# The banded-attention section issued two steps at a time, with its value and score matmuls next to each other

## The chip, the cores and the metric

The kernel runs on one core of a Trainium2 chip. The metric is device time in microseconds (us), from one execution; lower is better. TensorE does the matmuls, VectorE, ScalarE and GpSimd work beside it, and SyncE issues the loads of the weights. Each engine takes its instructions in the order in which they are written, and waits for the others by semaphores.

## The reference

The program is a whole model: two layers of one kind of block, then two layers of another. The change touches one part, the attention of the last layer, which looks 128 tokens to either side (512 tokens, 16 query heads, 4 key heads, head width 64, float32):

```python
def window_gqa_mixer(h, wqkv, wo, sink, cos, sin):
    qkv = h @ wqkv
    ...
    o, _ = band_attention(q, k, v, B_RADIUS, B_BLOCK, sink.reshape(B_KV_HEADS, grp))
    return o.reshape(b, s, B_HEADS * D_HEAD) @ wo

# band_attention, for one query block of 128 and its neighbours
s = jnp.einsum('nbqhgd,nbkhd->nbhgqk', qb, kb) * (dh ** -0.5)
s = jnp.where(valid, s, NEG_INF)
m = jnp.maximum(jnp.max(s, axis=-1), sk)
pr = jnp.exp(s - m[..., None])
den = jnp.sum(pr, axis=-1) + jnp.exp(sk - m)
o = jnp.einsum('nbhgqk,nbkhd->nbqhgd', pr, vb) / den
```

## The kernel before

The section (`mixer_b`) has two kinds of work for TensorE. The *dense* work multiplies the 512 tokens by weights: a tile of 128 outputs takes 8 pieces (4 in the last phase), a piece is three matmuls of 512 columns (L913 to L915), and the weights of each 8 pieces are a *unit*. The first 96 pieces make the tiles k0, v0, q0, q1, k1, q2, q3, v1, q4 to q7; the next 32 are the first half of the output projection. When a tile is done, VectorE takes it out of its bank: a rope tile by a shuffle and a product (L2704, L2705), after which GpSimd does two more operations on it (L842, L843). At the end of each unit ScalarE makes the high part of a later unit's weights (L1645) and VectorE the low part (L2146).

The *banded* work is 32 steps `s` of two heads (`g` = 0, 1) and one query tile `t = s % 4`. `b_blocks(s)` gives its key blocks: two at t = 0 and 3, three at t = 1 and 2. A step has these stages:

- `scores`: TensorE, one float32 matmul for each head, 256 or 384 columns, on 64 rows of the array each, into banks 2 and 3 (even s) or 4 and 5 (odd s); then VectorE adds the mask, takes the row maximum (L2746) and makes the bias of the exponential (L2827).
- `exps`: ScalarE, one exponential for each head, in place in `scb` (L2033).
- `norm`: VectorE, a reciprocal (L2770) and two scalings (L2772).
- `blocks`: TensorE transposes (L1537) into the one bank 6, four of them in one group at two key blocks, two groups of three at three; ScalarE copies each group to `ptb` (L2059), and the next group waits for that copy.
- `values`: TensorE, 8 or 12 instructions (L1551), 64 columns of the array for each head, into bank 7. After every fourth step ScalarE and VectorE take bank 7 out in two parts (`out`, `out_lo`).

The order is written out by hand in the generator `plan_b` (L304), which every engine walks for itself, taking the stages that are its own. `dense.send(n)` issues n pieces, with the events "unit" and "part" where a unit or a half tile ends. Before step 0, 46 pieces are out; the 32 steps issue the other 82. In front of the loop VectorE still takes out tile k1 behind `scores` 1. `rest` (the second half of the output projection) follows.

`ptb` is one buffer, so that a copy waits for the values of the step before; `scb` and the small statistics have three.

Of the kernel before, what the change touches and what calls it, by code (L numbers as in the profile page):

```python
# [21 lines left out]
ALU = mybir.AluOpType  # L22
# [281 lines left out]
def plan_b():  # L304


    dense = woven(len(B_TILES), B_PART, lambda d: B_TILES[d][0] == "v", BY_THREE)
    next(dense)
    yield from dense.send(40)
    yield "scores", 0  # L310
    yield "exps", 0
    yield from dense.send(3)
    yield "norm", 0
    yield "scores", 1
    yield from dense.send(3)
    for s in range(32):
        if s % 4 == 0 and s:
            yield "out_lo", s // 4 - 1
        if s == 0:
            yield "blocks", (0, 0)  # L320
            yield "exps", 1
        if s < 30:
            yield "scores", s + 2
        if s:
            yield "blocks", (s, 0)
        if s < 31:
            yield "norm", s + 1
        n = 3 if s % 3 and s not in (25, 28, 31) else 2
        if len(b_blocks(s)) == 3:
            yield from dense.send(1)  # L330
            yield "blocks", (s, 1)
            yield from dense.send(n - 1)
        else:
            yield from dense.send(n)
        if s < 30:
            yield "exps", s + 2
        yield "values", s
        if s % 4 == 3:
            yield "out", s // 4
# [70 lines left out]
def build(nc, stream, x_t, p_t, small, vecs, tab1, tab_a, tab_b, consts, out):  # L410
    n_units = stream.shape[0]
    with ExitStack() as ctx:
# [81 lines left out]
        scb = [at(f"scb{i}", [P, 2, 3 * P + 8], offset=o + i * (6 * P + 16) * 4) for i in range(3)]; o += 3 * (6 * P + 16) * 4  # L494
        ptb = at("ptb", [P, 6 * P], offset=o); o += 6 * P * 4
# [16 lines left out]
        mxs = at("mxs", [P, 3, 2, 2])  # L512
        nms = at("nms", [P, 3, 2])
        dns = at("dns", [P, 3, 2])
        rdn = at("rdn", [P, 3, 2])
        nsink = at("nsink", [P, 16])
        sink8 = at("sink8", [P, 16])
        eps = at("eps", [P, 2])
# [132 lines left out]

        def b_scores(s, g):

            return scb[s % 3][:, g, (3 - len(b_blocks(s))) * P:3 * P]

        block = ctx.enter_context(nc.Block())

# [249 lines left out]
        def _(pe):  # L907
# [621 lines left out]
            def blocks_b(s, i):  # L1529

                nb = len(b_blocks(s))
                if i == 0:
                    c.wait(p_scaled)
                dst = group_bank()
                for j in range(4 if nb == 2 else 3):
                    g, k = divmod(j, 2) if nb == 2 else (i, j)
                    mm = pe.transpose(dst[:, chunk(j)], b_scores(s, g)[:, chunk(k)], ident[:, :])  # L1537
                mm.then_inc(grp_done, 1)

            def values_b(s):  # L1540

                qc, t = divmod(s, QT)
                nb = len(b_blocks(s))
                pe.wait_ge(grp_read, c.n["group"])
                if t == 0:
                    pe.wait_ge(o_lo, 4 + qc)
                if s == 0:
                    evicted(4)
                for k, kt in enumerate(b_blocks(s)):
                    for g in range(2):  # L1550
                        mm = pe.matmul(bank[7][rows(g), chunk(t)], bv[qc // 4][:, kt, rows(g)], ptb[:, chunk(nb * g + k)],  # L1551
                                       start=k == 0, stop=k == nb - 1, skip_group_check=True)
                mm.then_inc(v_done, 1)

# [77 lines left out]
        def _(act):  # L1632
# [358 lines left out]
            def exps_a(s):  # L1991

                act.wait_ge(m_ready, s + 1)
                for g in range(2):
                    sc = sca[s % 2][:, g, :]
                    act.activation(sc, sc, ACT.Exp, bias=nms[:, s % 3, g:g + 1], scale=0.125,
                                   accum_out=dns[:, s % 3, g:g + 1]).then_inc(e_done, 1)

            def mixer_a():
                c.start(banks_mixer)  # L2000
# [27 lines left out]
            def exps_b(s):  # L2028

                act.wait_ge(m_ready, 16 + s + 1)  # L2030
                for g in range(2):
                    sc = scb[s % 3][:, g, (3 - len(b_blocks(s))) * P:3 * P + 1]
                    act.activation(sc, sc, ACT.Exp, bias=nms[:, s % 3, g:g + 1], scale=0.125,  # L2033
                                   accum_out=dns[:, s % 3, g:g + 1]).then_inc(e_done, 1)

            def mixer_b():
                c.start(banks_mixer)
                for stage, k in plan_b():
                    if stage == "unit":
                        unit_over()  # L2040
                        if k < len(B_TILES):
                            c.next_tile()
                        split_after(k, AFTER_NORM)
                    elif stage == "part":
                        c.next_tile()
                    elif stage == "turn":
                        c.tick("group")
                        act.wait_ge(grp_done, c.n["group"])
                        act.activation(bv[int(B_TILES[k][1])][:, :, :], bank[6][:, :].rearrange("p (t d) -> p t d", t=QT),
                                       ACT.Copy).then_inc(grp_read, 1)  # L2050
                    elif stage == "exps":
                        exps_b(k)
                    elif stage == "blocks":
                        s, i = k
                        w = (4 if len(b_blocks(s)) == 2 else 3) * P
                        c.tick("group")
                        act.wait_ge(grp_done, c.n["group"])
                        act.wait_ge(v_done, 16 + s)
# [78 lines left out]
        def _(dve):  # L2137
# [612 lines left out]
            def scores_a(s):  # L2750

                if s == 0:
                    c.wait(mask_in, 16)
                dve.wait_ge(s_done, s + 1)
                if s >= 2:
                    dve.wait_ge(grp_done, c.n[f"step{s - 2}"])
                for g in range(2):
                    masked(sca[s % 2][:, g, 0:S], bank[2 + g][:, :], tba[:, A_M0 + s % QT * S:A_M0 + s % QT * S + S],
                           mxs[:, s % 3, g, 0:1])
                    masked(sca[s % 2][:, g, S:S + 2 * P], bank[4 + g][:, 0:2 * P], tba[:, A_M1:A_M1 + 2 * P],  # L2760
                           mxs[:, s % 3, g, 1:2])
                for g in range(2):
                    ins = dve.tensor_scalar(nms[:, s % 3, g:g + 1], mxs[:, s % 3, g, 0:1], mxs[:, s % 3, g, 1:2], -0.125,
                                            ALU.max, ALU.mult)
                ins.then_inc(m_ready, 1)

            def norm(s, n, sc):

                dve.wait_ge(e_done, 2 * (n + s + 1))
                link(dve.reciprocal(rdn[:, s % 3, :], dns[:, s % 3, :]))  # L2770
                for g in range(2):
                    ins = dve.tensor_scalar(sc(g), sc(g), rdn[:, s % 3, g:g + 1], None, ALU.mult)  # L2772
                ins.then_inc(p_scaled, 1)

            def mixer_a():
# [36 lines left out]
            def scores_b(s):  # L2812

                qc, t = divmod(s, QT)
                nb = len(b_blocks(s))
                h0 = qc // 4 * 8 + qc % 4
                if s == 0:
                    c.wait(mask_in, 16)
                dve.wait_ge(s_done, 16 + s + 1)
                if s >= 3:  # L2820
                    dve.wait_ge(grp_done, c.n[f"step{s - 3}"])
                dve.tensor_reduce(scb[s % 3][:, :, 3 * P], sink8[:, h0:h0 + 5:4].unsqueeze(2), AX.X, ALU.max)
                for g in range(2):
                    masked(b_scores(s, g), bank[2 + 2 * (s % 2) + g][:, 0:nb * P],
                           tbb[:, B_M + (b_blocks(s)[0] - t + 1) * P:B_M + (b_blocks(s)[0] - t + 1 + nb) * P],
                           mxs[:, s % 3, g, 0:1])
                dve.scalar_tensor_tensor(nms[:, s % 3, :], mxs[:, s % 3, :, 0], -0.125, nsink[:, h0:h0 + 5:4],  # L2827
                                         ALU.mult, ALU.min).then_inc(m_ready, 1)

            def mixer_b():  # L2830
# [281 lines left out]
```

## Time and profile before

| | us |
|---|---|
| median of 3 runs | 3358.89 (3358.5 to 3358.99) |
| the profiled execution | 3358.6 |
| its span in the profile | 3356.6 |

| engine | busy, us of the span |
|---|---|
| TensorE (PE) | 3310.1 |
| VectorE (DVE) | 1818.7 |
| ScalarE (ACT) | 1244.5 |
| GpSimd (POOL) | 332.5 |

Times in the profile are microseconds from the first instruction. The length of a matmul in it includes a tail that overlaps the next one, so what a matmul costs is read from one start to the next start. The 32 banded steps run from 2765.09 us (transposes of step 0) to 2895.29 us (first piece of `rest`), 130.20 us.

### The profile page before, as it was taken

The numbers are of one execution on the slowest core, as the hardware profiler recorded it, in microseconds if no ns is written. First come the engines' busy times: TensorE is split into PE (matmuls) and PEld (weight loads), VectorE is DVE, ScalarE is ACT, GpSimd is POOL, SyncE is SP. The second block draws the span as 40 slices with busy tenths as digits, with TensorE's granted clock in tenths as the row PEclk, the third lists the DMA queues.
The fourth block names the chain that finished last, engine by engine and source line by source line (L and its number), as shares of the span: only waits on it lengthen the run. The fifth ranks groups of instructions, "written<-read, shape, count | busy, mean of one in ns | idle before, by whom it ended". The sixth has DMA issues, their size and how long they took to land.

```text
span 3356.6 us, 43153 instructions
## 1 busy us (share of the span) xinstructions
PE 3310.1 (99%) x16870; PEld 2645.2 (79%) x16870; DVE 1818.7 (54%) x2946; ACT 1244.5 (37%) x1882; POOL 332.5 (10%) x242
## 2 busy tenths in 40 slices
PE   9999999999999999999999999999999999999999
PEld 7767888776788878888777778888888876788887
DVE  6776333677743446443666664436644367654436
ACT  3355232425532324232333343224433235532325
POOL 0300000231100020000223100001000012000001
PEclk9999999999999999999999999999999999999999
DMA  4112222321122222223322122233222321132332
GB/s 166 63 45 80 96 95 99 126 69 45 62 96 95 100 94 84 98 94 107 109 70 70 64 88 94 100 102 106 82 94 100 102 96 45 57 107 94 100 107 82
DMA packets 81433, 300.39 MB, mean 89 GB/s; under 512 B 9040, under 2 KB 9040, under 8 KB 80640
## 3 DMA queue, kind: packets, MB, share of 16 engines
q1 hardware_dynamic: 78624, 284.20, 25.2%
q0 software_dynamic: 1568, 11.98, 0.9%
q8 instruction: 105, 1.72, 0.2%
q10 hardware_dynamic: 1088, 2.10, 0.2%
q14 instruction: 48, 0.39, 0.0%
HBM read 296.14 MB, written 2.10 MB: 89 GB/s over the span
## 4 chain that ended last, share of the span: by engine, by line
PE 90%; DVE 4%; ACT 3%; issue 1%; POOL 1%; DMA 0%; POOLq 0%; ACTq 0%; DVEq 0%
PE bank L913 26%; PE bank L915 25%; PE bank L914 25%; PE bank L957 2%; PE bank L964 2%; PE bank L958 2%; PE bank L1241 1%; PE bank L1222 1%; PE bank L1482 1%; PE bank L1494 1%; DVE wl L2146 1%; ACT wh L1645 1%; PE bank L1537 1%; ACT sc L1817 1%; PE bank L1256 1%
## 5 line engine op out<-in xcount | busy, mean ns | idle before, releaser
L913 PE MATMUL bank<-x,wh 128*128 128x512 f32 x2616 | 1043.9, 399 | 3.1 <-DVE wl L2146 1.8
L915 PE MATMUL bank<-x,wl 128*128 128x512 f32 x2616 | 1020.0, 390 | 0.0
L914 PE MATMUL bank<-x,wh 128*128 128x512 f32 x2616 | 1018.8, 389 | 0.0
L1645 ACT ACTIVATE wh<-raw 128x1024 fp32r<-128x1024 f32 x526 | 556.8, 1059 | 1114.5 <-PE bank L915 1062.5
L2146 DVE TENSOR_TENSOR wl<-raw,wh 128x1024 fp32r<-128x1024 f32 x526 | 669.9, 1274 | 534.0 <-ACT wh L1645 533.1
L913 PEld LDWEIGHTS bank<-x,wh 128*128 128x128 f32 x2616 | 491.3, 188 | 122.5 <-issue 22.6
L915 PEld LDWEIGHTS bank<-x,wl 128*128 128x128 f32 x2616 | 491.0, 188 | 104.2
L914 PEld LDWEIGHTS bank<-x,wh 128*128 128x128 f32 x2616 | 491.8, 188 | 99.3 <-issue 3.8
L913 PE MATMUL bank<-mid,wh 128*128 128x512 f32 x1216 | 474.9, 391 | 0.5 <-DVE wl L2146 0.5
L914 PE MATMUL bank<-mid,wh 128*128 128x512 f32 x1216 | 473.1, 389 | 0.0
L915 PE MATMUL bank<-mid,wl 128*128 128x512 f32 x1216 | 473.1, 389 | 0.0
L913 PEld LDWEIGHTS bank<-mid,wh 128*128 128x128 f32 x1216 | 228.3, 188 | 49.7 <-DVE wl L2146 1.3
L914 PEld LDWEIGHTS bank<-mid,wh 128*128 128x128 f32 x1216 | 228.3, 188 | 48.4 <-issue 1.0
L915 PEld LDWEIGHTS bank<-mid,wl 128*128 128x128 f32 x1216 | 228.3, 188 | 47.1
L2290 DVE TENSOR_TENSOR prod<-bank,rs_in 128x512 f32<-128x512 f32 x88 | 60.8, 691 | 233.2 <-PE bank L915 233.2
L2162 DVE TENSOR_TENSOR mid<-prod,mid 128x512 f32 (+1 forms) x152 | 104.8, 689 | 89.7 <-ACT mid L1958 86.9
L710 POOL TENSOR_TENSOR acc<-sq,sq 128x512 f32<-128x512 f32 x8 | 11.2, 1396 | 1283.9 <-ACT sq L1762 1283.9
L2628 DVE TENSOR_TENSOR prod<-tmp,bank 128x512 f32<-128x512 f32 x64 | 44.0, 687 | 142.7 <-ACT tmp L1908 142.7
L1958 ACT ACTIVATE mid<-prod 128x512 f32 (+1 forms) x88 | 55.8, 634 | 174.7 <-DVE prod L2676 174.7
L1908 ACT ACTIVATE tmp<-bank 128x512 f32<-128x512 f32 x64 | 38.3, 598 | 177.9 <-PE bank L915 177.9
L957 PE MATMUL bank<-x,wh 128*128 128x512 f32 x200 | 80.3, 401 | 13.5 <-DVE wl L2146 7.0
L2290 DVE TENSOR_TENSOR tmp<-bank,rs_in 128x512 f32<-128x512 f32 x88 | 60.8, 691 | 56.9 <-PE bank L915 55.8
(377 smaller groups left out, 3323.3 us busy)
## 6 DMA issues: line engine op xcount, KB each, us to landing
raw<-stream SPq DMA_DIRECT2D x526, 512.0 KB, 3.2
raw_apart<-stream SPq DMA_DIRECT2D x12, 512.0 KB, 3.6
sm<-small POOLq DMA_DIRECT2D x2, 2144.0 KB, 9.7
tb<-tab POOLq DMA_DIRECT2D x2, 1728.0 KB, 13.9
h<-x_t ACTq DMA_DIRECT2D x4, 512.0 KB, 6.8
out_t<-h SPq DMA_DIRECT2D x8, 256.0 KB, 2.7
tba<-tab_a POOLq DMA_DIRECT2D x1, 1152.0 KB, 8.1
pf<-p_t POOLq DMA_DIRECT2D x2, 512.0 KB, 5.4
```

Source lines behind the costliest of these rows:

```text
L913: pe.matmul(dst, hi, src[:, kc, 0, :], start=start, stop=False)
L914: pe.matmul(dst, hi, src[:, kc, 1, :], start=False, stop=False)
L915: return pe.matmul(dst, lo, src[:, kc, 0, :], start=False, stop=stop)
L957: pe.matmul(dst, hi, x[:, kc, 0, :], start=kc == 0, stop=False)
L958: pe.matmul(dst, lo, x[:, kc, 0, :], start=False, stop=False)
L964: mm = pe.matmul(dst, hi, x[:, kc, 1, :], start=False, stop=kc == 7)
L1645: act.activation(high_of(n)[:, :], raw_of(n)[:, :], ACT.Copy).then_inc(hi_done, 1)
L1958: act.activation(mid[:, i * 2 + k, 0, :], prod[k][:, :], ACT.Copy).then_inc(mid_hi, 1)
L2146: dve.tensor_tensor(low_of(n)[:, :], raw_of(n)[:, :], high_of(n)[:, :].bitcast(F32), ALU.subtract).then_inc(split_done, 1)
L2162: dve.tensor_tensor(dst, src, hi.bitcast(F32), ALU.subtract).then_inc(done, 1)
L2290: free(dve.tensor_tensor(dst, bank[c.peek()][:, :], rs_in[:, :], ALU.mult))
L2628: free(dve.tensor_tensor(prod[k % 2][:, :], tmp[k % 2][:, :], b[:, :], ALU.mult))
```

## The change

The loop of `plan_b` takes two steps in a pass. A pass has three transpose groups. The first comes at its start; behind it the values of both steps of the pass *before*, the scores of both steps of the *next* pass, then 1 piece (2 in four passes), the second group, 2 pieces, the third group, 2 pieces. The exponentials of the next two steps are placed behind the second and third group, their norms in front of the last two pieces and behind them. Norm 1 moves behind scores 2 and 3. The last two steps' values come behind the loop. `scb`, `ptb` and the statistics have four buffers, and the waits follow them. The arithmetic is the same.

```diff
-    for s in range(32):
-        if s % 4 == 0 and s:
-            yield "out_lo", s // 4 - 1
-        if s == 0:
-            yield "blocks", (0, 0)
-            yield "exps", 1
-        if s < 30:
-            yield "scores", s + 2
-        if s:
-            yield "blocks", (s, 0)
-        if s < 31:
-            yield "norm", s + 1
-        n = 3 if s % 3 and s not in (25, 28, 31) else 2
-        if len(b_blocks(s)) == 3:
-            yield from dense.send(1)
-            yield "blocks", (s, 1)
-            yield from dense.send(n - 1)
-        else:
-            yield from dense.send(n)
-        if s < 30:
-            yield "exps", s + 2
-        yield "values", s
-        if s % 4 == 3:
-            yield "out", s // 4
+    for s in range(0, 32, 2):
+        groups = [(i, g) for i in (s, s + 1) for g in range(len(b_blocks(i)) - 1)]
+        yield "blocks", groups[0]
+        if s == 0:
+            yield "exps", 1
+        else:
+            yield "values", s - 2
+            yield "values", s - 1
+            if s % 4 == 0:
+                yield "out", s // 4 - 1
+        for i in range(s + 2, min(s + 4, 32)):
+            yield "scores", i
+        if s == 0:
+            yield "norm", 1
+        elif s % 4 == 0:
+            yield "out_lo", s // 4 - 1
+        few = 2 * s % 3 == 1 and s < 24
+        yield from dense.send(2 if few else 1)
+        yield "blocks", groups[1]
+        if s < 30:
+            yield "exps", s + 2
+        yield from dense.send(2)
+        yield "blocks", groups[2]
+        if s < 30:
+            yield "exps", s + 3
+            yield "norm", s + 2
+        yield from dense.send(2)
+        if s < 30:
+            yield "norm", s + 3
+    yield "values", 30
+    yield "values", 31
+    yield "out", 7
...
-                pe.wait_ge(grp_read, c.n["group"])
+                pe.wait_ge(grp_read, c.n[f"turned{s}"])
...
-                        act.wait_ge(v_done, 16 + s)
-                        act.activation(ptb[:, i * w:i * w + w], bank[6][:, 0:w], ACT.Copy).then_inc(grp_read, 1)
+                        if s >= 4:
+                            act.wait_ge(v_done, 16 + s - 3)
+                        act.activation(ptb[s % 4][:, i * w:i * w + w], bank[6][:, 0:w], ACT.Copy).then_inc(grp_read, 1)
...
-                if s >= 3:
-                    dve.wait_ge(grp_done, c.n[f"step{s - 3}"])
+                if s >= 4:
+                    dve.wait_ge(grp_done, c.n[f"step{s - 4}"])
```

## Rows read from the trace of the kernel before

**Rows 1.** The page, part 1: busy time of each engine over the whole span.
```profile
PE 3310.1 (99%) x16870; PEld 2645.2 (79%) x16870; DVE 1818.7 (54%) x2946; ACT 1244.5 (37%) x1882; POOL 332.5 (10%) x242
```

**Rows 2.** Windows view, the 32 steps: stretch, length, engine busy (instructions), clock, DMA share, GB/s.
```profile
2765.09:2895.29 130.20, 126.71 (x852) 84.08 (x850) 96.73 (x323) 75.46 (x191) 24.64 (x15) 1.00 0.12 41
```

**Rows 3.** Timeline of TensorE: start, length, line, operands, count, wait before. Steps 3 to 6.
```profile
2780.77 0.40 PE L915 MATMUL bank<-x,wl 128*128 128x512 f32 x1
2781.10 0.66 PE L1551 MATMUL bank<-ptb,bv 128*64 128x128 f32 x8
2781.69 0.92 PE L1525 MATMUL bank<-bk,bq 64*128 64x384 f32 x4
2782.53 0.66 PE L1537 MATMUL bank<-ident,scb 128*128 128x128 f32 x4
2782.95 0.48 PE L913 MATMUL bank<-x,wh 128*128 128x512 f32 x1
...
2790.20 0.88 PE L1551 MATMUL bank<-ptb,bv 128*64 128x128 f32 x12
2791.01 0.70 PE L1525 MATMUL bank<-bk,bq 64*128 64x256 f32 x4
2791.64 0.55 PE L1537 MATMUL bank<-ident,scb 128*128 128x128 f32 x3
2791.94 0.47 PE L913 MATMUL bank<-x,wh 128*128 128x512 f32 x1
2792.26 0.39 PE L914 MATMUL bank<-x,wh 128*128 128x512 f32 x1
2792.48 0.40 PE L915 MATMUL bank<-x,wl 128*128 128x512 f32 x1
2792.77 0.55 PE L1537 MATMUL bank<-ident,scb 128*128 128x128 f32 x3
```

**Rows 4.** The same view at step 0, where scores follow transposes.
```profile
2765.09 0.60 PE L1537 MATMUL bank<-ident,scb 128*128 128x128 f32 x4
2765.62 0.92 PE L1525 MATMUL bank<-bk,bq 64*128 64x384 f32 x4
```

**Rows 5.** Timeline of VectorE around step 0, and the TensorE instruction that waits for it.
```profile
2765.32 0.72 DVE L2704 STREAM_SHUFFLE prod<-bank 128x512 f32<-128x512 f32 x1
2766.53 1.21 DVE L2146 TENSOR_TENSOR wl<-raw,wh 128x1024 fp32r<-128x1024 f32 x1
2767.67 0.14 DVE L2822 TENSOR_REDUCE scb<-sink 128x2 f32<-128x2 f32 x1
2768.99 0.16 DVE L2770 RECIPROCAL rdn<-dns 128x2 f32<-128x2 f32 x1
...
2769.99 0.55 PE L1537 MATMUL bank<-ident,scb 128*128 128x128 f32 x3 [0.64 <-DVE scb L2772]
```

**Rows 6.** Timeline of VectorE, scores of 256 columns up to the reciprocal behind them.
```profile
2791.76 0.16 DVE L2822 TENSOR_REDUCE scb<-sink 128x2 f32<-128x2 f32 x1 [2.69 <-PE bank L1525]
...
2792.83 0.16 DVE L2770 RECIPROCAL rdn<-dns 128x2 f32<-128x2 f32 x1
```

**Rows 7.** Timeline of ScalarE: high part of a unit's weights, exponential, copy of a group.
```profile
2781.21 1.06 ACT L1645 ACTIVATE wh<-raw 128x1024 fp32r<-128x1024 f32 x1 [0.79 <-PE bank L915]
2782.17 0.60 ACT L2033 ACTIVATE scb<-scb,nms 128x385 f32<-128x385 f32 x1
...
2788.91 0.49 ACT L2059 ACTIVATE ptb<-bank 128x384 f32<-128x384 f32 x1 [0.64 <-PE bank L1537]
```

**Rows 8.** Timelines of GpSimd and VectorE, rope operations meeting VectorE's.
```profile
1726.43 1.30 POOL L842 TENSOR_TENSOR prod<-prod,tba 128x512 f32<-128x512 f32 x1 [5.94 <-DVE aq L2705]
1727.81 2.15 POOL L843 TENSOR_TENSOR aq<-aq,prod 128x512 f32<-128x512 f32 x1
...
1727.06 1.75 DVE L2146 TENSOR_TENSOR wl<-raw,wh 128x1024 fp32r<-128x1024 f32 x1 [0.71 <-ACT wh L1645]
...
2776.83 1.66 DVE L2772 TENSOR_SCALAR scb<-scb,rdn 128x256 f32<-128x256 f32 x2
```

More of the change, by code:

```diff
@@ L493, in build @@
         tbb = at("tbb", [P, B_N], offset=o); o += B_N * 4
-        scb = [at(f"scb{i}", [P, 2, 3 * P + 8], offset=o + i * (6 * P + 16) * 4) for i in range(3)]; o += 3 * (6 * P + 16) * 4
-        ptb = at("ptb", [P, 6 * P], offset=o); o += 6 * P * 4
+        scb = [at(f"scb{i}", [P, 2, 3 * P + 8], offset=o + i * (6 * P + 16) * 4) for i in range(4)]; o += 4 * (6 * P + 16) * 4
+        ptb = [at(f"ptb{i}", [P, 6 * P], offset=o + i * 6 * P * 4) for i in range(4)]; o += 4 * 6 * P * 4
         o += (x_at - o) % 512
@@ L511, in build @@
         dnc = at("dnc", [P, 2, QT])
[L512 to L515, printed above, removed]
+        mxs = at("mxs", [P, 4, 2, 2])
+        nms = at("nms", [P, 4, 2])
+        dns = at("dns", [P, 4, 2])
+        rdn = at("rdn", [P, 4, 2])
         nsink = at("nsink", [P, 16])
@@ L652, in b_scores @@
         def b_scores(s, g):
-            return scb[s % 3][:, g, (3 - len(b_blocks(s))) * P:3 * P]
+            return scb[s % 4][:, g, (3 - len(b_blocks(s))) * P:3 * P]
         block = ctx.enter_context(nc.Block())
@@ L1538, in blocks_b @@
                 mm.then_inc(grp_done, 1)
+                c.n[f"turned{s}"] = c.n["group"]
             def values_b(s):
@@ L1550, in values_b @@
                     for g in range(2):
-                        mm = pe.matmul(bank[7][rows(g), chunk(t)], bv[qc // 4][:, kt, rows(g)], ptb[:, chunk(nb * g + k)],
+                        mm = pe.matmul(bank[7][rows(g), chunk(t)], bv[qc // 4][:, kt, rows(g)], ptb[s % 4][:, chunk(nb * g + k)],
                                        start=k == 0, stop=k == nb - 1, skip_group_check=True)
@@ L1995, in exps_a @@
                     sc = sca[s % 2][:, g, :]
-                    act.activation(sc, sc, ACT.Exp, bias=nms[:, s % 3, g:g + 1], scale=0.125,
-                                   accum_out=dns[:, s % 3, g:g + 1]).then_inc(e_done, 1)
+                    act.activation(sc, sc, ACT.Exp, bias=nms[:, s % 4, g:g + 1], scale=0.125,
+                                   accum_out=dns[:, s % 4, g:g + 1]).then_inc(e_done, 1)
             def mixer_a():
@@ L2031, in exps_b @@
                 for g in range(2):
-                    sc = scb[s % 3][:, g, (3 - len(b_blocks(s))) * P:3 * P + 1]
-                    act.activation(sc, sc, ACT.Exp, bias=nms[:, s % 3, g:g + 1], scale=0.125,
-                                   accum_out=dns[:, s % 3, g:g + 1]).then_inc(e_done, 1)
+                    sc = scb[s % 4][:, g, (3 - len(b_blocks(s))) * P:3 * P + 1]
+                    act.activation(sc, sc, ACT.Exp, bias=nms[:, s % 4, g:g + 1], scale=0.125,
+                                   accum_out=dns[:, s % 4, g:g + 1]).then_inc(e_done, 1)
             def mixer_b():
@@ L2758, in scores_a @@
                     masked(sca[s % 2][:, g, 0:S], bank[2 + g][:, :], tba[:, A_M0 + s % QT * S:A_M0 + s % QT * S + S],
-                           mxs[:, s % 3, g, 0:1])
+                           mxs[:, s % 4, g, 0:1])
                     masked(sca[s % 2][:, g, S:S + 2 * P], bank[4 + g][:, 0:2 * P], tba[:, A_M1:A_M1 + 2 * P],
-                           mxs[:, s % 3, g, 1:2])
+                           mxs[:, s % 4, g, 1:2])
                 for g in range(2):
-                    ins = dve.tensor_scalar(nms[:, s % 3, g:g + 1], mxs[:, s % 3, g, 0:1], mxs[:, s % 3, g, 1:2], -0.125,
+                    ins = dve.tensor_scalar(nms[:, s % 4, g:g + 1], mxs[:, s % 4, g, 0:1], mxs[:, s % 4, g, 1:2], -0.125,
                                             ALU.max, ALU.mult)
@@ L2769, in norm @@
                 dve.wait_ge(e_done, 2 * (n + s + 1))
-                link(dve.reciprocal(rdn[:, s % 3, :], dns[:, s % 3, :]))
+                link(dve.reciprocal(rdn[:, s % 4, :], dns[:, s % 4, :]))
                 for g in range(2):
-                    ins = dve.tensor_scalar(sc(g), sc(g), rdn[:, s % 3, g:g + 1], None, ALU.mult)
+                    ins = dve.tensor_scalar(sc(g), sc(g), rdn[:, s % 4, g:g + 1], None, ALU.mult)
                 ins.then_inc(p_scaled, 1)
@@ L2819, in scores_b @@
                 dve.wait_ge(s_done, 16 + s + 1)
-                if s >= 3:
-                    dve.wait_ge(grp_done, c.n[f"step{s - 3}"])
-                dve.tensor_reduce(scb[s % 3][:, :, 3 * P], sink8[:, h0:h0 + 5:4].unsqueeze(2), AX.X, ALU.max)
+                if s >= 4:
+                    dve.wait_ge(grp_done, c.n[f"step{s - 4}"])
+                dve.tensor_reduce(scb[s % 4][:, :, 3 * P], sink8[:, h0:h0 + 5:4].unsqueeze(2), AX.X, ALU.max)
                 for g in range(2):
@@ L2825, in scores_b @@
                            tbb[:, B_M + (b_blocks(s)[0] - t + 1) * P:B_M + (b_blocks(s)[0] - t + 1 + nb) * P],
-                           mxs[:, s % 3, g, 0:1])
-                dve.scalar_tensor_tensor(nms[:, s % 3, :], mxs[:, s % 3, :, 0], -0.125, nsink[:, h0:h0 + 5:4],
+                           mxs[:, s % 4, g, 0:1])
+                dve.scalar_tensor_tensor(nms[:, s % 4, :], mxs[:, s % 4, :, 0], -0.125, nsink[:, h0:h0 + 5:4],
                                          ALU.mult, ALU.min).then_inc(m_ready, 1)
```

## The prediction

> **What bounds the kernel now.** I read the page's busy times first: TensorE works for 3310.1 of 3356.6 us [rows 1]. What the change can win is a shorter sequence on TensorE itself, or one of its waits; what it can lose is a new wait. Then the windows view of the 32 steps: 126.71 of 130.20 us busy, so only 3.49 us of waits are there to be won, at the full clock (1.00, the 2.4 GHz level) [rows 2]. VectorE is busy for 96.73 us of it and ScalarE for 75.46: neither is the bound, but both are full enough that the *place* of an operation in their queues decides when it is ready. Last the timelines, read from one start to the next start.
>
> **What one kind of matmul behind another costs** [rows 3, 4]. Dense behind dense: 0.22 or 0.23 (2792.26 to 2792.48). Values: 8 instructions 0.59, 12 take 0.81, so 0.055 each and a pause of 0.15 before what follows. Scores: 384 columns 0.84, 256 columns 0.63, so 0.21 for 128 columns, 0.64 of work in 384 and a pause of 0.20. Dense to values 0.33 and dense to transposes 0.29: pauses of 0.10 and 0.06. The first dense matmul behind transposes 0.32: a pause of 0.09. Four transposes 0.42 before dense, 0.53 before scores: 0.11.
>
> **The sequence (a gain).** Removed: the pause between the values of a pair (16 x 0.15 = 2.4), that between the scores of a pair (15 x 0.20 = 3.0), dense to values (32 x 0.10 = 3.2), 16 of the 48 first dense matmuls behind transposes (16 x 0.09 = 1.4). Together 10.0. Added: transposes to values, not in the trace; nearest are transposes to scores, 0.11, and dense to values, 0.10. I take 0.11, 16 x = 1.8 (nothing at one end, at the other the largest pause seen, 0.20: 3.2). Dense to transposes in 47 groups instead of 16: 31 x 0.06 = 1.9. Dense behind scores, taken as behind transposes: 15 x 0.09 = 1.3. Together 5.0. The net gain is 5.0 us. The number of pieces (128), transposes and copies stays. That values of two steps follow each other without a pause is not in the trace either: between 0 and 0.15 each, for scores between 0 and 0.20. I take 0, because the instructions inside a step follow each other at 0.055; the other end costs 5.4 us.
>
> The Trainium skill speaks against that choice: "TensorE: Matmul & The Clock Gate", section "Part 3: Packing small matmuls — row/col tiling", says that a weight load overlaps matmuls in flight only where it goes to other row groups, and the second step's loads go to the first one's. By that rule the sequence would gain about nothing; by the rows it gains 5.0.
>
> **The old waits (a gain).** All 3.49 us go where nothing takes their place. The added buffers cost nothing: values now wait for a copy made half a pass before. GpSimd's rope of k1 waits for norm 1 and starts later; it is needed only by scores 8. SyncE's loads wait for units, which end at most a few us later than now, with three units loaded ahead.
>
> **The start: norm 1 moved behind scores 3 (a loss).** VectorE's queue at step 0 is tile k1 (2765.32), a split (2766.53), scores 2 (2767.67, 1.32 long), norm 1 (2768.99); the transposes of step 1 start 1.00 behind that, at 2769.99, after 0.64 of waiting [rows 5]. Now scores 3 (256 columns, 1.07 [rows 6]) lie in between, so the group can start at 2768.99 + 1.07 + 1.00 = 2771.06. TensorE has less work ahead of it: transposes 0.53, scores 0.64 + 0.43 + 0.20, one piece with its pauses 0.84; it is there at 2767.73. Wait: 3.3 us. All dense work stands behind it on TensorE. In the same pass tile q2 (piece 48) ends in front of norm 2. Taking it out (1.21) and a split (1.14) [rows 5] precede the norm: piece 48 ends 1.3 behind 2771.06, then 1.21 + 1.2 + 1.0 make 4.7, while TensorE has only 3.65 of work (two groups 0.61, four pieces 2.76, pauses 0.3). Wait: 1.05.
>
> **A pass, and where a unit ends in it.** Times from the pass's first transposes, s % 4 = 0. TensorE: group 0.53, values 1.07 + 0.16, scores until 3.03, one piece, second group at 3.9, third at 5.7, next pass at 7.5. VectorE: scores from 2.7 to 5.1, `out_lo` to 5.75. ScalarE: second group's transposes over at 4.45 (0.55 long), its copy (0.49) done about 4.85, two exponentials of 0.60 [rows 7] to 6.1; the norm is then ready at 7.2, 0.3 to spare. With s % 4 = 2 it has 0.8 to spare. Without a unit's end nothing waits.
>
> Where a unit ends ahead of norm s + 2, VectorE must first take the tile out (1.21, or about half for a tile without rope) and split, and the split waits for ScalarE's high part, 0.96 (2781.21 to 2782.17 [rows 7]), which lies behind the exponentials. The pieces out when the passes begin are 46, 51, 57, 62, 67, 73, 78, 83, 89, 94, 99, 105, 110, 115, 120, 125. So units end ahead of norm s + 2 in passes 0, 6, 12, 18 and 24, and behind it in 2, 8, 14, 20 and 26.
> - Pass 24 (no rope): exponentials to 6.1, high part to 7.1, split to 8.3, norm ready at 9.3 instead of 7.5: wait 1.75.
> - Pass 12 (q5): the same without GpSimd. Pass 18 (q7; no `out_lo`, 256 columns): 8.85, wait 1.3.
> - Pass 6 (v1): its turn is due at the very end of the pass, and the next transposes wait for that copy out of bank 6: 1.15.
> - End: the copy for values 31 stands behind a unit's high part, and values 30 hide only part of it: 0.6.
>
> **GpSimd comes between** [rows 8]. Its L842 ran from 1726.43 to 1727.73. VectorE's split, due at 1727.06, took 1.75 instead of 1.21 [rows 5]: it began when GpSimd ended. L843 then waited for the split and ended at 1729.96, 3.53 behind L842's start. A norm of 256 columns took 1.66 at 2776.83, most of it blocked. So where the rope of a tile, its split and a norm meet, the norm is ready about 3.53 + 0.8 behind GpSimd's start. Pass 12: tile out at 7.1, ready 11.45, wait 3.95. Pass 18: 6.4, wait 3.15. In passes 2, 8 and 14 it delays norm s + 3 and VectorE's next scores: 1.5, 0.7 and 1.5.
>
> New waits: 3.3 + 1.05 + 1.5 + 1.15 + 0.7 + 3.95 + 1.5 + 3.15 + 1.75 + 0.6 = 18.65 us. Total: 3358.6 + 18.65 - 3.49 - 5.0 = 3368.8 us, against the profiled execution's own time; the median of the runs lies 0.3 above that.
>
> **Rivals.**
> - *GpSimd does not get in between* (VectorE's split runs before the rope asks, or the norm goes first): waits 3.3 + 1.05 + 1.15 + 1.75 + 1.3 + 1.75 + 0.6 = 10.9, time 3361.0, not slower by what can be told. It decides by the order of the two requests; in pass 12 both are due at 7.1, within 0.1 us. Against it: [rows 8]. 0.22.
> - *The new waits hardly exist*, since exponentials and splits come earlier than I read: under 1.8 us of them, time under 3352. The queue in [rows 5] speaks against it. 0.06.
> - *The new neighbours keep their pauses*: 5.4 more, 3374.2. 0.12.
> - *The clock falls in the 3.3 us wait.* The steps ran at the full clock with 3.49 us of waits in all, in several pieces [rows 2]; a wait this long is not in them. A dense matmul at 1.2 GHz would take twice its 0.23, an estimate, so two pieces and a group behind the wait lose about 1.7: 3370.5. 0.13. The Trainium skill, "TensorE: Matmul & The Clock Gate", section "Why this matters for your kernels", warns of such gaps between bursts of matmuls.
> - The forecast: 0.47; of that 0.07 falls within 0.2%, since five terms of over 1 us rest on an order read by hand.
>
> **How the numbers follow.** 0.2% (6.7 us) is about what a measurement can tell from no change. Slower: 0.40 + 0.12 + 0.13 = 0.65. Same: 0.22 + 0.07 = 0.29. Faster: 0.06. The range leaves out the fastest case and the tops of the slowest, and most of what lies below 3361: 3359 to 3375.
>
> **What would show it.** TensorE waiting for L2772 for some 3.3 us near 2771; waits of 1 to 4 us at the start of passes 8, 14, 20 and 26; the two scores of a pair within 1.27 us up to the next dense piece instead of 1.47; about 140 us for the stretch that took 130.20. Wrong if TensorE's waits for L2772 sum to under 10 us, or if pairs keep the old pauses.

## The result, and the profile after

| | before | after |
|---|---|---|
| median of 7 runs, us | 3358.67 (3358.5 to 3358.99) | 3371.64 (3367.1 to 3372.34) |
| the profiled execution, us | 3358.6 | 3372.06 |
| its span, us | 3356.6 | 3370.1 |
| the 32 banded steps, us | 130.20 | 144.08 |
| of that TensorE busy, us | 126.71 | 127.32 |
| granted clock in the steps | 1.00 | 0.94 |

The ratio of after to before is 1.0035, with a 95% interval of 1.0024 to 1.0047: slower by 13.0 us. That is inside the range (3359 to 3375), in the direction forecast, and 2.8 us above the predicted 3368.8. The runs of after also lie further apart (5.2 us) than those of before (0.5 us). In experiments 1, 2 and 10 one or two runs had a lower granted clock over the whole kernel (0.65 to 0.78) and took 18 to 41% longer; the medians given below are those of the other runs, as the ratios are.

All of it lies in the banded steps. The page's busy time of TensorE, 3311.0 us (98%) where it was 3310.1 (99%) [rows 1], says nothing of the loss. The windows view does, and answers to [rows 2]. Its columns are the stretch, its length, the busy time (instructions) of PE, PEld, DVE, ACT and POOL, the granted clock, the DMA share and GB/s. First come the 32 steps, then four short stretches, each directly behind one of TensorE's longest waits:

```profile
2765.24:2909.32 144.08, 127.32 (x851) 93.90 (x849) 103.97 (x324) 72.84 (x191) 23.46 (x15) 0.94 0.12 40
2771.23:2774.46 3.23, 3.23 (x9) 2.57 (x10) 1.01 (x3) 2.30 (x6) 2.56 (x2) 0.51 0.09 11
2830.03:2835.62 5.59, 5.59 (x31) 3.68 (x31) 1.72 (x9) 0.49 (x1) 0.00 (x0) 0.50 0.00 0
2860.27:2863.44 3.17, 3.17 (x24) 2.67 (x24) 0.76 (x3) 0.60 (x1) 0.00 (x0) 0.54 0.00 0
2886.13:2890.75 4.62, 4.62 (x31) 3.08 (x31) 1.54 (x8) 0.49 (x1) 0.00 (x0) 0.63 0.01 4
```

Idle time of TensorE rose from 3.49 us to 144.08 - 127.32 = 16.76. Busy time rose by 0.61 only because two things cancel: a shorter sequence, and stretches at half the clock. The view of the waits in the steps, one line for each pair of waiter and releaser (total, times, longest), says on what TensorE waits. L2782 is the norm's scaling (L2772 before), L1545 the transposes:

```profile
PE bank L1545 <- DVE scb L2782: 15.2, 10, 3.5
PE bank L1545 <- ACT bv L2058: 1.0, 1, 1.0
PE bank L1560 <- ACT ptb L2069: 0.4, 1, 0.4
```

The start of the section in TensorE's timeline (start, length, line, tiles, the idle time in front). Behind the wait the first dense matmul (L921) takes 0.57 to the next start, where 0.32 is usual [rows 3]:

```profile
2771.23 0.90 PE L1545 MATMUL bank<-ident,scb 128*128 128x128 f32 x3 [3.22 <-DVE scb L2782]
2771.78 0.78 PE L921 MATMUL bank<-x,wh 128*128 128x512 f32 x1
2772.35 0.63 PE L922 MATMUL bank<-x,wh 128*128 128x512 f32 x1
```

And a pass in which nothing waits, the same view. A group of three between dense pieces, then the pass's first group, the values (L1560) of two steps and the scores (L1533) of two:

```profile
2781.07 0.39 PE L923 MATMUL bank<-x,wl 128*128 128x512 f32 x1
2781.30 0.49 PE L1545 MATMUL bank<-ident,scb 128*128 128x128 f32 x3
2781.54 0.48 PE L921 MATMUL bank<-x,wh 128*128 128x512 f32 x1
...
2784.84 0.60 PE L1545 MATMUL bank<-ident,scb 128*128 128x128 f32 x4
2785.37 1.31 PE L1560 MATMUL bank<-ptb,bv 128*64 128x128 f32 x20
2786.61 1.35 PE L1533 MATMUL bank<-bk,bq 64*128 64x384 f32 x8
2787.89 0.50 PE L921 MATMUL bank<-x,wh 128*128 128x512 f32 x1
```

From start to start: values of both steps 1.24, scores of both 1.28, as costed (1.23, and 1.27); there is one pause for the two, not one for each.

The longest wait, before pass 14, has VectorE and GpSimd in it. Their timelines in the last 4 us ahead of it (L2156 is the split, L850 and L851 are GpSimd's rope, L842 and L843 before):

```profile
2826.07 1.23 DVE L2156 TENSOR_TENSOR wl<-raw,wh 128x1024 fp32r<-128x1024 f32 x1
2827.40 2.57 DVE L2782 TENSOR_SCALAR scb<-scb,rdn 128x384 f32<-128x384 f32 x2
...
2826.19 2.23 POOL L850 TENSOR_TENSOR prod<-prod,tbb 128x512 f32<-128x512 f32 x1 [10.84 <-DVE bq L2715]
2828.49 1.26 POOL L851 TENSOR_TENSOR bq<-bq,prod 128x512 f32<-128x512 f32 x1
```

L850 asks at 2826.19 while the split runs, and ends 1.1 behind it, at 2828.42. The norm's two scalings, 0.75 elsewhere, take 2.57: the first (2827.40 to 2828.63) is held until L850 has ended, the second (2828.55 to 2829.97) until L851 has (2829.75). The transposes follow at 2830.03, 3.54 late, and they, the values and the scores run at about half the clock (TensorE's timeline):

```profile
2830.03 0.90 PE L1545 MATMUL bank<-ident,scb 128*128 128x128 f32 x3 [3.54 <-DVE scb L2782]
2830.86 2.40 PE L1560 MATMUL bank<-ptb,bv 128*64 128x128 f32 x20
2833.19 2.51 PE L1533 MATMUL bank<-bk,bq 64*128 64x256 f32 x8
```

### The profile page after: what moved, and what is told of

It is laid out like the page before. It is cut to its first block, busy times and chain, and to the rows that moved or that the text cites. A ratio compares the mean times of both kernels' runs of the same rounds, so it can differ in the third digit from the quotient of the medians.

```text
span 3370.1 us, 43146 instructions
## 1 busy us (share of the span) xinstructions
PE 3311.0 (98%) x16870; PEld 2655.9 (79%) x16870; DVE 1825.3 (54%) x2946; ACT 1238.8 (37%) x1882; POOL 331.2 (10%) x242
## 4 chain that ended last, share of the span: by engine, by line
PE 90%; DVE 5%; ACT 3%; issue 1%; POOL 1%; DMA 0%; POOLq 0%; DVEq 0%; ACTq 0%
PE bank L921 26%; PE bank L923 25%; PE bank L922 25%; PE bank L965 2%; PE bank L972 2%; PE bank L966 2%; DVE wl L2156 1%; PE bank L1249 1%; PE bank L1230 1%; ACT wh L1654 1%; PE bank L1490 1%; PE bank L1502 1%; ACT sc L1826 1%; PE bank L1264 1%; PE bank L1560 1%
## 5 line engine op out<-in xcount | busy, mean ns | idle before, releaser
L921 PE MATMUL bank<-x,wh 128*128 128x512 f32 x2616 | 1044.6, 399 | 3.1 <-DVE wl L2156 1.7
L2156 DVE TENSOR_TENSOR wl<-raw,wh 128x1024 fp32r<-128x1024 f32 x526 | 673.7, 1282 | 538.8 <-ACT wh L1654 537.7
L921 PEld LDWEIGHTS bank<-x,wh 128*128 128x128 f32 x2616 | 491.6, 188 | 127.1 <-issue 27.0
L921 PE MATMUL bank<-mid,wh 128*128 128x512 f32 x1216 | 474.9, 391 | 0.5 <-DVE wl L2156 0.5
L921 PEld LDWEIGHTS bank<-mid,wh 128*128 128x128 f32 x1216 | 228.3, 188 | 49.5 <-DVE wl L2156 1.3
L965 PE MATMUL bank<-x,wh 128*128 128x512 f32 x200 | 80.5, 403 | 13.3 <-ACT x L1788 6.8
```

The lines of the kernel that those rows point to most:

```text
L921: pe.matmul(dst, hi, src[:, kc, 0, :], start=start, stop=False)
L965: pe.matmul(dst, hi, x[:, kc, 0, :], start=kc == 0, stop=False)
L2156: dve.tensor_tensor(low_of(n)[:, :], raw_of(n)[:, :], high_of(n)[:, :].bitcast(F32), ALU.subtract).then_inc(split_done, 1)
```

## The experiments

The first four take the changed kernel apart, and their diffs are against it. The next three build a version without the late norms, and the last three price the sequence on that version.

**1. Norm 1 back in front of scores 2 and 3.** Is the start's wait the place of norm 1 in VectorE's queue?

```diff
-        for i in range(s + 2, min(s + 4, 32)):
-            yield "scores", i
         if s == 0:
             yield "norm", 1
-        elif s % 4 == 0:
+        for i in range(s + 2, min(s + 4, 32)):
+            yield "scores", i
+        if s % 4 == 0 and s:
             yield "out_lo", s // 4 - 1
```

> Norm 1 goes back in front of scores 2 and 3 in VectorE's queue; all else as in the changed kernel. Theory (the order in VectorE's queue makes the wait at the start, and the wait makes the clock fall): TensorE's wait before the transposes of step 1 shrinks from 3.3 us to about 0.9, matmuls behind it stay 0.23 us apart instead of 0.43, a wait of about 2 us appears before the transposes of step 2 since scores 2 and 3 now precede tile q2, and the time falls by about 3.8 us (2.3 of wait, 1.5 of clock), to about 3368. Rival (exponential 1 or the copy of the first group sets that wait): the wait stays near 3.3 us, the time is that of the changed kernel.

Measured: 3369.6 us (3367.87 to 3370.73), ratio 1.0032 (1.002 to 1.0044). TensorE's timeline at the starts of the second group of pass 0, of pass 2 and of pass 20:

```profile
2769.03 0.55 PE L1545 MATMUL bank<-ident,scb 128*128 128x128 f32 x3 [0.82 <-DVE scb L2782]
...
2775.02 0.55 PE L1545 MATMUL bank<-ident,scb 128*128 128x128 f32 x3 [2.32 <-DVE scb L2782]
...
2857.39 0.65 PE L1545 MATMUL bank<-ident,scb 128*128 128x128 f32 x4 [3.12 <-DVE scb L2782]
```

The wait of 3.22 became 0.82. But norm 2 still stands behind a tile and a split, and the wait before pass 2 grew from 0.45 to 2.32. Together they fell from 3.67 to 3.14, so most of the gain of 2.0 us is likely that the clock kept its full rate here (the group's 0.55 is the full-clock length), which in after cost 1.46 us more. The profiled execution, the fastest of these runs, gained 4.2 us: in it the clock stayed full (1.00) behind the wait of 3.12 before pass 20 too, where it fell behind 3.10 in after. A wait shortened in front of a second, independent one mostly moves it.

**2. Norm s + 2 directly behind its exponentials**, ahead of the dense pieces' tiles and splits in VectorE's queue.

```diff
             yield "exps", s + 2
+            yield "norm", s + 2
         yield from dense.send(2)
         yield "blocks", groups[2]
         if s < 30:
             yield "exps", s + 3
-            yield "norm", s + 2
```

> Norm s+2 stands directly behind exponential s+2, ahead of the pieces in which a unit can end; all else as in the changed kernel. Theory (a tile taken out and a split in front of the norm make the waits of 3.7, 3.2 and 1.9 us at the start of passes 14, 20 and 26): these three and the 0.6 us before pass 2 go, with the half-rate stretches behind them (2.6, 1.4 and 1.6 us); the waits at pass 0 (3.3 us), pass 8 (1.05 us, bank 6 for v1's turn) and passes 4, 12 and 16 (norm s+3 behind a rope) stay. Time about 3371.6 - 9.4 - 5.6 = 3356.6. Rival (exponential s+2 is what comes late, not the unit in front of it): the waits stay, time near 3371. Third view (the waits move: VectorE is late for the scores or tiles instead): the three go, but others of 1 us or more appear, time 3360 to 3366.

Measured: 3358.6 us (3358.22 to 3359.28), ratio 0.9999 (0.9989 to 1.0009): 13.0 us less than after, and level with before. The waits on a norm in the steps:

```profile
PE bank L1545 <- DVE scb L2782: 6.4, 6, 3.2
```

Those before passes 2, 14, 20 and 26 are gone; the start's 3.20 stays. So the late place of one norm was the largest part of the loss.

**3. GpSimd kept away.** Tiles q3 to q7 get their rope on GpSimd only once a later norm is over.

```diff
-BEHIND_NORM = {3: 0, 4: 1, 5: 2}
+BEHIND_NORM = {3: 0, 4: 1, 5: 2, 6: 5, 8: 11, 9: 14, 10: 17, 11: 20}
```

> GpSimd's rope of tiles q3, q4, q5, q6, q7 waits for norm 5, 11, 14, 17 and 20 too; nothing is moved on the other engines. Theory (GpSimd's two operations get between the split and the norm, about 1.9 us each time): the waits at passes 14 and 20 shrink from 3.7 and 3.2 us to about 1.75 and 1.3, those before the second group of passes 4 and 16 (1.1 us each) and before pass 12 (0.8 us) go, the one at pass 26 (1.9 us, no rope there) stays. Waits fall by about 7 us and the half-rate stretches behind passes 14 and 20 by up to 4: time 3361 to 3365. Rival (ScalarE's high part, not GpSimd, makes the split late): no wait shrinks, time near 3371.

Measured: 3361.49 us (3358.88 to 3362.41), ratio 1.0006 (0.9996 to 1.0015). The same places as in the last section, VectorE, GpSimd, and TensorE before passes 14, 20 and 26:

```profile
2826.09 0.75 DVE L2782 TENSOR_SCALAR scb<-scb,rdn 128x384 f32<-128x384 f32 x2
...
2826.92 1.27 POOL L850 TENSOR_TENSOR prod<-prod,tbb 128x512 f32<-128x512 f32 x1 [10.54 <-DVE scb L2782]
...
2826.90 0.55 PE L1545 MATMUL bank<-ident,scb 128*128 128x128 f32 x3 [1.74 <-DVE scb L2782]
...
2851.70 0.66 PE L1545 MATMUL bank<-ident,scb 128*128 128x128 f32 x4 [1.27 <-DVE scb L2782]
...
2876.23 0.55 PE L1545 MATMUL bank<-ident,scb 128*128 128x128 f32 x3 [1.75 <-DVE scb L2782]
```

The scalings take 0.75 instead of 2.57, and the waits before passes 14 and 20 are 1.74 and 1.27 where they were 3.54 and 3.10. These are the values that the prediction's first rival gave for a GpSimd that stays out (1.75 and 1.3), so GpSimd's part is shown. The waits in the steps fell from 16.6 to 11.0 us, and behind passes 14 and 20 no half-clock stretch follows (some 4 us): 9.6 of the 10.2 us gained.

**4. TensorE kept working in the four long waits.** The fillers write into bank 6, which the transposes overwrite; no wait on the norm is touched.

```diff
+AWAKE_B = {(1, 0): 14, (14, 0): 14, (20, 0): 13, (26, 0): 7}
...
+                        if k in AWAKE_B:
+                            pe.wait_ge(grp_read, c.n["group"])
+                            stay_awake(AWAKE_B[k], 6)
                         blocks_b(*k)
```

> Adds 14, 14, 13 and 7 small matmuls into bank 6 (their output is overwritten) before the first transposes of step 1 and of passes 14, 20 and 26, where TensorE waits 3.3, 3.7, 3.2 and 1.9 us; nothing is taken away. Theory (the idle time of TensorE lets the granted clock fall to 1.2 GHz, worth 1.5 + 2.6 + 1.4 + 1.6 = 7.1 us): the waits are filled, what follows them stays at 0.23 us per dense matmul, the clock of the whole run reads 1.00, the time falls by 5 to 7 us, to about 3365 to 3367, and the runs lie closer together than 3367.1 to 3372.3. Rival (the slow stretches come from something else, such as operands arriving late): they stay, and the time is the same or longer.

Measured: 3365.84 us (3365.38 to 3366.44), ratio 1.002 (1.0011 to 1.003): 5.8 us less than after. The windows view behind the start, and TensorE's timeline there (the fillers are L1020) and before pass 14:

```profile
2768.00:2776.00 8.00, 6.88 (x47) 5.77 (x46) 6.44 (x22) 3.99 (x11) 2.69 (x3) 1.00 0.20 67
```

```profile
2767.81 3.29 PE L1020 MATMUL bank<-ident,ones 128*128 128x128 f32 x28
2771.19 0.55 PE L1548 MATMUL bank<-ident,scb 128*128 128x128 f32 x3
...
2829.13 0.55 PE L1548 MATMUL bank<-ident,scb 128*128 128x128 f32 x3 [0.18 <-DVE scb L2788]
...
2832.13 0.50 PE L924 MATMUL bank<-x,wh 128*128 128x512 f32 x1
```

The transposes of step 1 start at 2771.19, as late as in after, but what follows has the clock 1.00. Before pass 14 the same 31 instructions take 2832.13 - 2829.13 = 3.00 us; in after they took 5.59. In after the four stretches cost 7.1 us (worked out below). The wait before pass 2 grew by 0.57, from 0.45 to 1.02, as TensorE now comes to it sooner; 7.1 less 0.57 is near the 6.45 us by which the two profiled executions differ, and the 5.8 of the medians. The runs also lie within 1.1 us of each other instead of 5.2. So the falls of the clock are a cost of their own, and the likely source of after's scatter.

**5 and 6. Two norms moved, then three.** The diff is against experiments 1 and 2 together, which are the kernel with two norms.

```diff
             yield "exps", s + 3
-        yield from dense.send(2)
-        if s < 30:
             yield "norm", s + 3
+        yield from dense.send(2)
```

> Norm 1 ahead of scores 2 and 3, and norm s+2 directly behind exponential s+2. Theory (the two orders act at different places, so their gains add): the wait before the transposes of step 1 is 0.8 us instead of 3.2, no wait before pass 2, no half-rate stretch at the start; the waits of 1.0, 0.2, 1.05, 0.7, 1.0 and 0.2 us at passes 4 to 18 stay. Time about 3358.8 - 2.4 - 1.0 = 3355.4, faster than the kernel before by 0.1%. Rival (what is taken from the start comes back, as it did when norm 1 alone was moved): near 3358.8.

> As the one before, and norm s+3 directly behind exponential s+3, ahead of the last pieces of the pass. Theory (the waits of 1.0 + 0.2 us at passes 4 and 16 and of 0.7 us at pass 12 are norm s+3 or the scores behind it, held up by a tile taken out, a split and GpSimd): all but the 1.05 us of v1's turn and the 0.8 us at the start go, 3.1 us less: about 3352.3, 0.2% faster than the kernel before. Rival (tiles are now taken out so late that the next scores on VectorE, or TensorE's free bank, wait): waits for L2837's consumers or for a bank appear, 3354 to 3357.

Measured: two norms 3356.2 us, ratio 0.9992 (0.9983 to 1.0001); three norms **3353.07** us (3352.7 to 3353.36), ratio 0.9982 (0.9973 to 0.9992), 5.7 us faster than before. Three norms, the window of the steps and TensorE's waits in them:

```profile
2765.02:2889.94 124.92, 119.69 (x852) 88.87 (x850) 99.75 (x324) 72.68 (x191) 23.73 (x15) 1.00 0.14 46
```

```profile
PE bank L1544 <- DVE scb L2781: 2.6, 4, 0.8
PE bank L1544 <- ACT bv L2057: 1.1, 1, 1.1
PE bank L920 <- DVE y L2734: 0.5, 1, 0.5
PE bank L1544 <- ACT ptb L2068: 0.5, 1, 0.5
PE bank L1559 <- ACT ptb L2068: 0.4, 1, 0.4
```

The full clock throughout, 5.2 us of waits, and 119.69 us of TensorE work where before has 126.71 [rows 2]. This is the changed order's own worth, undisturbed: 7.0 us.

**7. Three norms, and GpSimd kept away as in 3.** Has GpSimd a price left?

```diff
-BEHIND_NORM = {3: 0, 4: 1, 5: 2}
+BEHIND_NORM = {3: 0, 4: 1, 5: 2, 6: 5, 8: 11, 9: 14, 10: 17, 11: 20}
```

> As the one before, and GpSimd's ropes of q3 to q7 wait for norms 5, 11, 14, 17 and 20. Theory (with both norms ahead of the tile, GpSimd has nothing of the chain to get in front of): no change, 3352.3 within 0.5 us. Rival (GpSimd still holds up the bias or split behind the tile): 0.5 to 1.5 us less.

Measured: 3353.17 us, ratio 0.9984 (0.9975 to 0.9993), and the same waits. None. The 1.8 us that GpSimd's part took from each of two waits in experiment 3 were its price *ahead of a late norm*.

The last three are against three norms, and price the sequence. **8. The values of the two steps apart.**

```diff
             yield "values", s - 2
-            yield "values", s - 1
...
         yield from dense.send(2 if few else 1)
+        if s:
+            yield "values", s - 1
```

> As the kernel with three norms moved, but the values of step s-1 stand behind the first pieces instead of behind the values of step s-2, so that the pairs of values are undone. Theory (each change of the kind of matmul costs TensorE a pause): per pass the pause behind values, 0.15, that from dense to values, 0.10, and about 0.1 for the transposes behind them: 15 passes, 5 us more than the kernel with the three norms moved. Rival (values of two steps do not overlap anyway, the gain came from elsewhere): less than 2 us more.

Measured: 3356.19 us (3355.91 to 3356.55), 3.1 us more than three norms. A pass in TensorE's timeline:

```profile
2799.77 0.88 PE L1559 MATMUL bank<-ptb,bv 128*64 128x128 f32 x12
2800.57 1.35 PE L1532 MATMUL bank<-bk,bq 64*128 64x384 f32 x8
...
2803.11 0.40 PE L922 MATMUL bank<-x,wl 128*128 128x512 f32 x1
2803.43 0.66 PE L1559 MATMUL bank<-ptb,bv 128*64 128x128 f32 x8
2804.02 0.55 PE L1544 MATMUL bank<-ident,scb 128*128 128x128 f32 x3
```

Values 0.80 and 0.59 instead of 1.24 together, and 0.32 from dense to values instead of 0.23: 0.24 a pass, and 0.06 for the group behind them (0.30 from 2804.02 to the next dense, where 0.24 stands between dense). 15 passes make 4.5 (4.4 by TensorE's work in the steps, 124.07 instead of 119.69), less 1.2 us of waits that went (those on the norm 2.0 instead of 2.6, that on `y` gone): 3.3, and 3.1 measured.

**9. The third group one piece behind the second.**

```diff
-        yield from dense.send(2)
+        yield from dense.send(1)
         yield "blocks", groups[2]
...
-        yield from dense.send(2)
+        yield from dense.send(3)
```

> As the kernel with three norms moved (3353.1 us), but the third transpose group stands one piece behind the second instead of two, and three pieces follow it. Theory (a group costs 0.24 us and no pause ahead of it where the copy of the group before is long done, so that its weights are loaded beside the dense matmuls; 0.30 and a pause of 0.05 where the copy comes just in time, as for every second group of a three-block step in the kernel before): the third group starts 1.0 us behind the second, whose copy is done after 1.0 to 1.1 us; 0.1 us of pause and transposes and 0.1 of wait for each of 16 passes, 3 us more: about 3356. Rival (the shorter groups come from something else, such as the longer run of dense pieces ahead): no change.

Measured: 3352.78 us (3352.62 to 3353.09), ratio 0.9982 (0.9973 to 0.9992): 0.3 less, no more than the spread. In the timeline the pause is there:

```profile
2811.83 0.40 PE L922 MATMUL bank<-x,wl 128*128 128x512 f32 x1
2812.20 0.63 PE L1544 MATMUL bank<-ident,scb 128*128 128x128 f32 x4
...
2819.65 0.55 PE L1544 MATMUL bank<-ident,scb 128*128 128x128 f32 x3
```

In front of a third group of four it is 0.37 instead of 0.23; in front of one of three 0.28, and the group then takes 0.30 instead of 0.24. All in all TensorE's work in the steps is 121.31 us instead of 119.69, 1.6 more. The waits fell by some 1.8 (the five lines above sum to 5.1, here to 3.3). The two cancel, so the time alone says nothing of the pause; the expected loss did not come.

What the pause is can be read beside ScalarE, which copies the group before out of the same bank 6. Its copy here, and the one ahead of the group at 2792.77 in the kernel before [rows 3]:

```profile
2819.11 0.49 ACT L2068 ACTIVATE ptb<-bank 128x384 f32<-128x384 f32 x1 [1.90 <-PE bank L1544]
...
2792.22 0.49 ACT L2059 ACTIVATE ptb<-bank 128x384 f32<-128x384 f32 x1 [1.84 <-PE bank L1537]
```

The copies end at 2819.60 and 2792.71, and the groups start 0.05 us behind, at 2819.65 and 2792.77; so do all 16 second groups of a step in before. (The group of four at 2812.20 starts 0.14 behind its copy.) With three norms that distance is 0.69 us or more at every group between dense pieces, and there is no pause. It is thus a wait for the copy, too short for the views to list as one, and no cost of going from dense matmuls to transposes.

**10. The scores of the two steps apart.**

```diff
-        for i in range(s + 2, min(s + 4, 32)):
-            yield "scores", i
+        if s < 30:
+            yield "scores", s + 2
...
         yield from dense.send(2 if few else 1)
+        if s < 30:
+            yield "scores", s + 3
```

> As the kernel with three norms moved (3353.1 us), but scores s+3 stand behind the first pieces of the pass, so that the pairs of scores are undone. Theory (the second step's scores follow the first one's without a pause, although their weights go to the same rows of the array): apart, each pass pays the pause behind scores, 0.20, one of about 0.1 from dense to scores and about 0.06 at the transposes behind; 15 passes, 5 us more, about 3358, less 0.3 at the start if the wait there takes it up. Rival (a score's weights cannot be loaded while another score runs on the same rows, so pairing saves nothing): 1 us more at most.

Measured: 3356.05 us (3355.76 to 3356.55), ratio 0.9992 (0.9982 to 1.0002), 3.0 us more than three norms. The timeline:

```profile
2817.00 0.92 PE L1534 MATMUL bank<-bk,bq 64*128 64x384 f32 x4
2817.85 0.50 PE L922 MATMUL bank<-x,wh 128*128 128x512 f32 x1
...
2818.43 0.40 PE L924 MATMUL bank<-x,wl 128*128 128x512 f32 x1
2818.75 0.70 PE L1534 MATMUL bank<-bk,bq 64*128 64x256 f32 x4
2819.39 0.55 PE L1546 MATMUL bank<-ident,scb 128*128 128x128 f32 x3
```

Scores 0.85 and 0.64 instead of 1.28, 0.32 instead of 0.23 in front of the second, and 0.06 for the group as in 8: 0.36 a pass, 5.4 for 15 (5.0 by TensorE's work in the steps, 124.70 instead of 119.69), less 2.0 us of waits (the norm's 1.2 instead of 2.6, `y` gone) make 3.0 to 3.4. Both steps' neighbours are thus worth about what the rows of before said.

## Why the prediction was right, and where it was not

The account of the 32 steps, forecast against measured. The parts of TensorE's work are sums of the distances from one start to the next, waits taken off, in the traces of before and of three norms, which has the same order of instructions on TensorE as after and the full clock throughout:

| | forecast, us | measured, us |
|---|---|---|
| scores (22.5 to 19.2) | -3.0 | -3.4 |
| values (22.3 to 20.1) | -2.4 | -2.2 |
| dense matmul in front of another kind (15.1 to 12.2) | -1.3 | -2.9 |
| transposes (17.0 to 17.6) | +1.8 | +0.6 |
| dense behind dense (49.8 to 50.7) | -0.1 | +0.9 |
| **sequence** | **-5.0** | **-7.0** |
| waits (3.49 to 16.76) | +15.2 | +13.3 |
| clock (127.32 - 119.69) | 0 | +7.6 |
| **together** | **+10.2** | **+13.9** |

- *The waits: right, place by place.* Start 3.3, measured 3.22. Pass 4 1.5, measured 0.99 and 0.22 before its second and third group. The turn of v1 1.15, measured 1.05. Pass 12 0.7, measured 0.72. Pass 14 3.95, measured 3.54. Pass 16 1.5, measured 0.99 and 0.21. Pass 20 3.15, measured 3.10. Pass 26 1.75, measured 1.74. End 0.6, measured 0.39. That a unit's end ahead of norm s + 2 costs and one behind it does not came out as read; experiment 2 took these waits away by that norm's place alone. Too high was the wait before pass 2: 1.05 forecast, 0.45 measured. There TensorE ran at half the clock behind the start's wait, so its work up to pass 2 took 1.46 longer, while piece 48, for which tile q2 waits, ended only some 0.9 later than costed (2.2 behind the group's start instead of 1.3). In experiment 4, with the full clock, this wait was 1.02.
- *GpSimd in between: right in size, wrong in the order.* The prediction had the tile's rope first and the split behind it. In pass 12 the split came first (2826.07 against 2826.19), and still the norm was as late, since GpSimd's first operation held the norm's first scaling and its second one the other. So the rival's condition, that VectorE's split runs before the rope asks, held there, and its lower wait did not come: the rival's reason was wrong too. In pass 18 the rope asked first, as forecast (2856.32, the split 2856.43). Experiment 3 shows what really decides: whether the rope is under way when the norm is.
- *The clock: the term that failed.* The prediction had it as a rival at 1.7 us for one wait, and left it out of the sum. It fell behind four. The sum itself held two more waits of over 3 us, before passes 14 and 20, and the rival priced neither. Even so the measured 3371.6 is nearer to the rival's 3370.5 than to the forecast 3368.8. Against the same instructions at the full clock, the four stretches cost 1.46 + 2.59 + 1.40 + 1.62 = 7.1 us (3.23 - 1.77, 5.59 - 3.00, 3.17 - 1.77, 4.62 - 3.00), 7.6 by the busy times of the table; experiment 4 gave 5.8 back, with 0.57 more of waiting before pass 2. The price of the first one, 1.7, was close to its 1.46. The Trainium skill, "TensorE: Matmul & The Clock Gate", section "Why this matters for your kernels", warns of idle gaps between bursts of matmuls. The trace agrees for these four waits, of which one was only 1.74, and not for the 3.12 us of experiment 1, behind which the clock stayed full.
- *The sequence: right in its main terms, 2.0 us too small.* The two paired kinds came out within 0.5 us, and experiments 8 and 10 confirm each alone. The failed step is "Dense to transposes in 47 groups instead of 16: 31 x 0.06 = 1.9". It took the 0.06 for the price of going from dense matmuls to transposes. It was a wait for ScalarE's copy out of bank 6, since in before one piece stands between the two groups of a step. Where the copy is long done there is no such pause (0.23), and the group itself takes 0.24 for three transposes instead of 0.30, 0.36 for four instead of 0.42; experiment 9 brings the short distance back, and with it 0.28 and 0.30. Against it, the pause from transposes to values was 0.17 (0.53 for four instead of 0.36) where 0.11 was taken, 1.0 more for 16, and dense work behind dense cost 1.0 more than forecast.
- *The rule weighed against the change* (the Trainium skill, "TensorE: Matmul & The Clock Gate", section "Part 3: Packing small matmuls — row/col tiling"), by which the sequence would have gained nothing, did not hold here. Two steps' scores on the same rows take 1.28, apart 0.85 + 0.64, and the sequence gained 7.0. The time shows that the pause goes; which weights were loaded when was not taken apart.
- *The nearness of the sum was partly luck.* Waits taken 1.9 us too high and a sequence taken 2.0 too small both made the forecast too long, by 3.9 together, and that hid about half of the 7.6 us of clock that it left out. What remained is 3.7 in the steps, and 2.8 between the predicted time and the median.

## What to carry to other kernels

When work on the bounding engine is regrouped, place each helper operation by where its *result is needed*, and then ask what its own queue puts in front of it: here 7.0 us of shorter sequence were won and 20.9 lost, and all but 1.7 of the loss went when the norms, 0.75 us each, stood directly behind what they depend on. Where such a wait falls on TensorE, price the clock behind it as a cost of its own: it fell behind 9 of the 12 waits of 1.7 us or more in after and experiments 1 to 3. And before a short pause is carried over as the price of a change of kind, see whether it ends just behind another engine's operation: then it is a wait, and goes or stays with that.

## What the runs showed of the hardware

- **The clock behind a wait.** It stood near the 1.2 GHz level behind waits of 3.22, 3.54, 3.10 and 1.74 us (granted 0.51, 0.50, 0.54, 0.63), in the stretches of 3.2 to 5.6 us shown above, and was back at 2.4 GHz behind them. The length of the wait does not decide alone: behind 2.32 and 3.12 us in experiment 1, and 1.74 and 1.27 in experiment 3, it stayed full (values of two steps 1.24), while in experiment 3 1.75 us before pass 26 brought it down (values 2.15, from 2876.71 to the scores at 2878.86). What tells these apart is open. Small matmuls during the four waits, into the bank that the transposes overwrite, kept it full behind all of them (experiment 4).
- **VectorE and GpSimd take turns in some operations.** Splits and scalings alternated with GpSimd's rope operations, one for one: two scalings of together 0.75 us took 2.57, the first behind the rest of one GpSimd operation, the second behind a whole one of 1.26. VectorE's mask operation, which reads a bank, was not held: with three norms it took its usual 0.42 at 2810.22 while L849 ran. The Trainium skill, "SBUF — State Buffer", section "Who interferes with whom", tells of a port that the two engines share under an exclusive lock; the trace agrees with that, and shows besides that two operations back to back in VectorE's queue do not keep GpSimd's from getting in between.
- **Small matmuls of different steps join without a pause**, even on the same rows of the array, as those inside a step do: values of two steps 1.24 us (apart 0.80 + 0.59), scores 1.28 (apart 0.85 + 0.64).
- **A bank's copy shows as a short pause**: 0.05 us lies between the end of ScalarE's copy and the next transposes into the bank where these stand ready, in all 16 second groups of before.
